# Product-key expert stages on one core: the first head's sixteen experts ranked and fetched as two groups of eight

## What is computed

```python
q = (h @ w_pq).reshape(B, L, PEER_HEADS, 2, PEER_QDIM // 2)
s = jnp.einsum("blhpd,hpkd->blhpk", q, peer_keys)
sv, si = lax.top_k(s, PEER_TOPK)
cand = (sv[..., 0, :, None] + sv[..., 1, None, :]).reshape(B, L, PEER_HEADS, PEER_TOPK * PEER_TOPK)
cidx = (si[..., 0, :, None] * N_KEYS + si[..., 1, None, :]).reshape(...)
top_s, pos = lax.top_k(cand, PEER_TOPK)
eidx = jnp.take_along_axis(cidx, pos, axis=-1)
gate = jax.nn.softmax(top_s, axis=-1)
a = jnp.einsum("tkd,td->tk", peer_down[ee], hh)
act = (gg * jax.nn.gelu(a)).astype(hh.dtype)
return jnp.einsum("tk,tkd->td", act, peer_up[ee])
```

## Time and profile before

| | us |
|---|---|
| three timed runs: median (lowest to highest) | 3960.98 (3959.01 to 3968.05) |
| span of the profiled execution, its own time from first to last instruction | 3961.4 |
| PE busy, matmuls (share) | 3596.4 (91%) |
| DVE busy | 2300.7 (58%) |
| ACT busy | 664.2 (17%) |
| POOL busy | 1284.5 (32%) |
| 16 DMA engines, mean rate | 304 GB/s |

### The profile page before, as it was taken

How to read it: one execution, slowest core, us unless ns; L and a number is a source line. 1 busy time by engine, 2 the same in 40 slices (tenths; PEclk the granted TensorE clock), 3 DMA queues, 4 the chain that set the end, 5 groups by cost and what they waited for, 6 DMA issues and landing times. The chain is left out here.

```text
span 3961.4 us, 41101 instructions
## 1 busy us (share of the span) xinstructions
PE 3596.4 (91%) x14600; PEld 2547.8 (64%) x14600; DVE 2300.7 (58%) x5460; ACT 664.2 (17%) x1814; POOL 1284.5 (32%) x1130
## 2 busy tenths in 40 slices
PE   8998999989999999999999989788779998877777
PEld 6667788878876888888847876333335786433333
DVE  3342013566877887765762147777763226777775
ACT  2232101110001330000002212111112211111111
POOL 1100000023445456774650013444341003444442
PEclk9999999999999999999999999899899999998999
DMA  8752345357998889998983259999996339999997
GB/s 331 291 202 89 128 149 191 128 207 291 345 354 343 292 296 412 406 400 343 414 353 132 102 221 411 398 414 407 411 419 274 108 126 375 405 419 419 420 419 327
DMA packets 206842, 1205.50 MB, mean 304 GB/s; under 512 B 23472, under 2 KB 24640, under 8 KB 95024
## 3 DMA queue, kind: packets, MB, share of 16 engines
q0 software_dynamic: 154976, 858.34, 54.0%
q1 hardware_dynamic: 51664, 344.55, 23.0%
HBM read 1201.64 MB, written 1.15 MB: 304 GB/s over the span
## 5 line engine op out<-in xcount | busy, mean ns | idle before, releaser
L1656 PE MATMUL bank<-big 128*128 128x256 f32 (+4 forms) x8888 | 1909.3, 374 | 47.3 <-DVE big L2435 13.8
L1656 PEld LDWEIGHTS bank<-big 128*128 128x128 f32 (+2 forms) x8888 | 1628.9, 190 | 338.3 <-issue 90.8
L2980 POOL DMA_INDIRECT big<-in_pboth,big x1024 | 1213.2, 1185 | 1301.0 <-PE bank L2134 703.7
L2134 PE MATMUL bank<-big 128*128 128x512 f32 x2048 | 990.6, 641 | 224.7 <-ACT big L2943 224.6
L2635 DVE CUSTOM_DVE_ANT_0 big<-big 128x1024 f32<-128x1024 f32 x768 | 926.1, 1223 | 338.6 <-DMA big<-in_pboth,big 333.2
L2134 PEld LDWEIGHTS bank<-big 128*128 128x128 f32 x2048 | 409.6, 204 | 785.8 <-issue 483.8
L2646 DVE SCALAR_TENSOR_TENSOR big<-big 128x1024 f32<-128x1024 f32 x254 | 326.1, 1284 | 75.7 <-DMA big<-in_pboth,big 55.3
L2967 POOL TENSOR_TENSOR big<-big 128x1 f32<-128x1 f32 (+1 forms) x49 | 42.4, 865 | 914.5 <-DVE big L2192 914.3
L2943 ACT ACTIVATE big<-big 128x128 f32<-128x128 f32 x512 | 165.4, 391 | 270.5 <-DVE big L2612 266.0
L2933 ACT ACTIVATE big<-big 128x4 f32<-128x4 f32 (+2 forms) x136 | 28.1, 207 | 730.9 <-DVE big L2608 725.6
L1836 PE MATMUL bank<-big 128*128 128x256 f32 x576 | 129.5, 378 | 0.0
(11 more groups left out here) (218 smaller groups left out, 2279.7 us busy)
## 6 DMA issues: line engine op xcount, KB each, us to landing
big<-in_w SPq DMA_DIRECT2D x104, 1024.0 KB
big<-in_wmod POOLq DMA_DIRECT2D x48, 1024.0 KB, 8.9
big<-in_wgu SPq DMA_DIRECT2D x44, 1024.0 KB
big<-in_wzg SPq DMA_DIRECT2D x36, 1024.0 KB, 4.8
big<-in_wro SPq DMA_DIRECT2D x32, 1024.0 KB
big<-in_wpq SPq DMA_DIRECT2D x24, 1024.0 KB, 4.9
big<-in_wd SPq DMA_DIRECT2D x22, 1024.0 KB
big<-in_pboth,big POOLq DMA_INDIRECT x1024, 11.0
```

Source lines behind the costliest of these rows:

```text
L1656: last = pe.matmul(o, a, b, start=(i == 0), stop=(i == n - 1))
L2134: last = pe.matmul(u.ap, d.ap, row[:, 512 * i:512 * i + 512], start=(k == 0), stop=(k == 127))
L2980: g.indirect_dma_start(out=s.ap, out_offset=None, in_=table, in_offset=bass.IndirectOffsetOnAxis(ap=index, axis=0)).then_inc(s.full[0], 16)
```

## The change

For head 0 of tile 0 in the expert stages of x (there `GH == 1`; the context's stage has `GH=8` and keeps its order) the 16 experts are ranked in two goes. First the eight best keys of either half are found, then the eight best of their 8 x 8 sums, then the row numbers of these eight, which the fetches of experts 0 to 7 wait for. After that the other eight keys of either half are found, and the sums, the 16 best and their row numbers are made as before; the last eight numbers are written, and the fetch of expert 8 waits for them. One more `next(route)` stands ahead of the steps of L1495, so that all steps of the old order follow as they were, behind the new first one.

```diff
         def rank(tt, h, sc, sc_ok, held=None):
+            eight = GH == 1 and tt == 0 and h == 0
+            keys = [dict(src=sc[:, p, :], vals=rk["sv"][:, p, :], idx=rk["si"].bitcast(U32)[:, p, :]) for p in range(2)]
+            if eight:
+                for p in range(2):
+                    put("rank_eight", ready=sc_ok if p == 0 else None, **keys[p])
+                ix_first.append(tick("index_done"))
+                put("rank_eight_index", rk=rk, dst=eix[0][:, 0, 0:8], done=ix_first[0])
+                yield 5
             for p in range(2):
-                put("rank_keys", src=sc[:, p, :], vals=rk["sv"][:, p, :], idx=rk["si"].bitcast(U32)[:, p, :],
-                    ready=sc_ok if p == 0 else None)
+                put("rank_others" if eight else "rank_keys", ready=sc_ok if p == 0 else None, **keys[p])
                 yield 1.8
             put("rank_pairs", tv=tvs[tt][:, h, :], rk=rk)
             yield 2.6
             ix_ok[tt][h] = tick("index_done")
-            put("rank_index", rk=rk, dst=[e[:, tt, 16 * h:16 * h + 16] for e in eix], done=ix_ok[tt][h])
+            put("rank_index", rk=rk, dst=[e[:, tt, 16 * h:16 * h + 16] for e in eix], done=ix_ok[tt][h], at=8 if eight else 0)
...
         asking = ask()
         route = ranks(asking)
+        next(route)
         next(route)
         r1 = stats(1, self.x_ok)
...
+                new = k % 16 == 0 or (tt, k) == (0, 8)
                 put("fetch", table=t["pboth"], s=s, index=eix[:, tt, k:k + 1],
-                    ready=ix_ok[tt][k // 16] if k % 16 == 0 else None, before=s.before)
+                    ready=ix_first[0] if tt + k == 0 else ix_ok[tt][k // 16] if new else None, before=s.before)
...
+    def rank_eight(src, vals, idx, ready):
+        settled()
+        if ready:
+            v.wait_ge(*ready)
+        step(v.max(vals[:, 0:8], src))
+        settled()
+        step(v.max_index(idx[:, 0:8], vals[:, 0:8], src))
+
+    def rank_others(src, vals, idx, ready):
+        settled()
+        step(v.match_replace(src, vals[:, 0:8], src, -3.0e38))
+        settled()
+        step(v.max(vals[:, 8:16], src))
+        settled()
+        step(v.max_index(idx[:, 8:16], vals[:, 8:16], src))
+
+    def rank_eight_index(rk, dst, done):
+        sv, ab, ia, iot = rk["sv"], rk["ab"][:, :, 0:8], rk["ia"][:, :, 0:8], rk["iot"][:, 0:8]
+        sf, tp = rk["sf"][:, :, 0:8], rk["tp"][:, 0:8]
+        c2 = rk["cand"].rearrange("p a b -> p (a b)")[:, 0:64]
+        oh = rk["oh"].rearrange("p a b -> p (a b)")[:, 0:128].rearrange("p (s k j) -> p s k j", s=2, k=8)
+        best8, abu = rk["ia"][:, 1, 8:16], ab.bitcast(U32)
+        settled()
+        step(v.tensor_tensor(c2.rearrange("p (a b) -> p a b", a=8), bc(sv[:, 0, 0:8], 8), bcm(sv[:, 1, 0:8], 8), ALU.add))
+        step(v.tensor_copy(sf, rk["si"].bitcast(U32)[:, :, 0:8]))
+        settled()
+        step(v.max(best8, c2))
+        settled()
+        step(v.max_index(tp, best8, c2))
+        settled()
+        step(v.tensor_scalar(abu[:, 0, :], tp, 3, None, ALU.logical_shift_right))
+        step(v.tensor_scalar(abu[:, 1, :], tp, 7, None, ALU.bitwise_and))
+        settled()
+        step(v.tensor_copy(ia, abu))
+        settled()
+        v.wait_ge(*rk["iot_ok"])
+        for s in range(2):
+            step(v.tensor_tensor(oh[:, s], bc(ia[:, s, :], 8), bcm(iot, 8), ALU.is_equal))
+        settled()
+        for s in range(2):
+            step(v.tensor_tensor(oh[:, s], oh[:, s], bcm(sf[:, s, :], 8), ALU.mult))
+        settled()
+        for s in range(2):
+            step(v.tensor_reduce(ab[:, s, :], oh[:, s], AX.X, ALU.add))
+        settled()
+        step(v.scalar_tensor_tensor(ia[:, 0, :], ab[:, 0, :], 128.0, ab[:, 1, :], ALU.mult, ALU.add))
+        settled()
+        step(v.tensor_scalar(ia[:, 0, :], ia[:, 0, :], float(16384 * rk["l"]), None, ALU.add))
+        settled()
+        v.tensor_copy(dst, ia[:, 0, :]).then_inc(done[0], 1)
+        v.wait_ge(*done)
+
...
-    def rank_index(rk, dst, done):
+    def rank_index(rk, dst, done, at):
...
-            v.tensor_copy(dst[0], ia[:, 0, :]).then_inc(done[0], 1)
+            v.tensor_copy(dst[0][:, at:16], ia[:, 0, at:16]).then_inc(done[0], 1)
         v.wait_ge(*done)
```

More of the change, by code:

```diff
@@ L1225, in routing @@
                   iot=iot, iot_ok=iot_ok, l=l)
-        ix_ok, gates_ok, ended = [[None] * 8 for _ in range(2)], {}, {}
+        ix_ok, gates_ok, ended, ix_first = [[None] * 8 for _ in range(2)], {}, {}, []
         def rank(tt, h, sc, sc_ok, held=None):
+            eight = GH == 1 and tt == 0 and h == 0
[6 more added lines that the diff above has]
+                yield 5
             for p in range(2):
-                put("rank_keys", src=sc[:, p, :], vals=rk["sv"][:, p, :], idx=rk["si"].bitcast(U32)[:, p, :],
-                    ready=sc_ok if p == 0 else None)
+                put("rank_others" if eight else "rank_keys", ready=sc_ok if p == 0 else None, **keys[p])
                 yield 1.8
@@ L1320, in route @@
             yield from first
-        return route, query, (score_begun, score_end), ranks, ix_ok, gates_ok, ended, query_tile
+        return route, query, (score_begun, score_end), ranks, ix_ok, gates_ok, ended, query_tile, ix_first
     def peer_queries(self, banks, sm, start, size, l, X, vec, ready, indices):
@@ L1355, in peer_c @@
         tvs = [kept.get(128, (8, 16)) for _ in range(2)]
-        route, _, _, ranks, ix_ok, gates_ok, _, _ = self.routing(ar, banks, wr, sm, l, 1, hT, hT_ok, tvs=tvs, gat=gat, eix=eix,
+        route, _, _, ranks, ix_ok, gates_ok, _, _, _ = self.routing(ar, banks, wr, sm, l, 1, hT, hT_ok, tvs=tvs, gat=gat, eix=eix,
                                                               qts=qts, GH=8, kept=kept, **rest)
@@ L1434, in peer_x @@
                              tvs=tvs, gat=gat, eix=[eix], qts=qts, GH=1)
-        _, query, (score_begun, score_end), ranks, ix_ok, gates_ok, ended, query_tile = parts
+        _, query, (score_begun, score_end), ranks, ix_ok, gates_ok, ended, query_tile, ix_first = parts
         yield "alone"
@@ L2676, in final @@
         v.scalar_tensor_tensor(X, X, by, fw, ALU.mult, ALU.mult).then_inc(normed[0], 1)
-    kinds = dict(consts=consts, block_consts=block_consts, row_stats=row_stats, row_turn=row_turn, dt=dt, dt_sums=dt_sums,
+    kinds = dict(consts=consts, rank_eight=rank_eight, rank_others=rank_others, rank_eight_index=rank_eight_index,
+                 block_consts=block_consts, row_stats=row_stats, row_turn=row_turn, dt=dt, dt_sums=dt_sums,
                  conv_in=conv_in, conv_end=conv_end, gate_in=gate_in, group_mask=group_mask, heads=heads, group_gate=group_gate, group_stats=group_stats,
```

## The result

The changed kernel takes **3972.22 us** (median of 15 runs, 3964.96 to 3979.49). The kernel before, run beside it on the same chip, takes 3963.7 (15 runs, 3956.85 to 3971.4). The ratio is **1.0021, 95% interval 1.0014 to 1.0028**: slower by 8.3 us, 5.5 to 11.1. The forecast of 3966.6 and its range up to 3971 were too low.

A forecast was written before the change was run, and what follows sets the result against it. PE was taken to bound about 120 us of each expert stage, started by DVE's ranking of head 0. Two stages at 2.8 us added 5.6, giving 3967.0 profiled, 3966.6 against the timed median; range 3959 to 3971.

The forecast's parts named there:

- the last one of the sum: Both expert stages: PE's run 3.3 us later, about 0.5 us to spare, so transfers 2.8 us later per stage.
- The 0.45 us: Second stage: fetch 46 is used 6.33 us after issue, 0.45 more than fetch 0, taken as its time to spare.
- the early fetches' cost: Start of a stage: fetches keep number, size and order, and the slots they take are free; no cost counted.
- The steps on DVE: Head 0's ranking: split adds nothing, the added index 3.3 us a stage (2.8 to 4.7), moving tile 1 back 3.3.
- What was won early is lost as a longer wait for slots: Expert stages: fetch 0 comes 3.45 us earlier, but later fetches wait for slots PE gives back, so nothing is gained.
- PE is the bound, the transfers follow it: First 120 us or so of a stage: PE has no gap and gives back slots; transfers follow by half a microsecond.
- the two falls of 2 us each: Sign in PE's run: the transfer rate falls to 283 GB/s at 3408 and 221 at 2470, read as transfers barely fed.
- The early start: Rival: transfers bound the whole stage, so each stage ends 3.45 us earlier, giving 3954.1 us; chance 0.08.
- It didn't cancel: Rival on PE's run: fetches have more to spare, for instance 3 us, so lateness cancels, giving 3961 us; chance 0.12.
- PE's clock: Rival: after longer idling PE's full clock returns late, head 1's query loses 3 us a stage, giving 3972.6; chance 0.10.
- a term whose own bounds went to +9.0: Lateness of both stages together: +5.6 us, from +3.2 at the lower price of the added index to +9.0 at the upper.

The follow-up runs named there:

- x1: Changed kernel with the first fetch waiting for head 0's full index, the index of eight still worked out but unused: 3972.46 us, ratio 1.0019.
- x2: Changed kernel with the row numbers of the first eight worked out twice, one after the other: 3977.7 us, ratio 1.0027.
- y1: Changed kernel with tile 1's way out of the banks right behind the first eight keys and the first fetch waiting for the full index: 3967.56 us, ratio 1.0006.
- y2: Kernel before with only tile 1's way out of the banks moved ahead of rank_index; no split ranking, no added instructions: 3968.2 us, ratio 1.0006.
- z2: x3 with the first fetch also waiting for the last DVE instruction of tile 1's way out, for which the query waits too: 3958.36 us, ratio 0.9984.
- x3: Changed kernel with tile 1's root between the eight keys and their index, its way out ahead of the second half's other keys: 3970.79 us, ratio 1.0018.
- z4: x3 with the ninth fetch waiting until tile 1's query on PE is complete, so eight fetches run ahead: 3964.55 us, ratio 1.0003.
- y3: x3 with the first fetch also waiting until tile 1's query on PE is complete: 3966.34 us, ratio 1.0005.
- z1: x3 with the third fetch waiting until tile 1's query on PE is complete, so two fetches run ahead: 3960.02 us, ratio 0.9988.
- z3: x3 with the sixth fetch waiting until tile 1's query on PE is complete, so five fetches run ahead: 3958.37 us, ratio 0.9988.

## Why the prediction was wrong

**The step that failed is the last one of the sum: that a fetch has 0.5 us to spare in each stage, to be taken off the 3.3, and that the transfers are 2.8 us later from there on.** The part before it held: PE's run starts 3.8 and 2.6 us later, 6.5 in all, and 2 x 3.3 was said. At the two fetches the lateness is still the forecast's, by the stages' ends it is not. Timeline of the changed kernel, POOL's fetch 47 of the first stage and DVE's use of it, and DVE's use of fetch 46 of the second; then fetch 46 of the second stage in the second profile of the kernel before:

```profile
2466.59 0.94 POOL L3042 DMA_INDIRECT big<-in_pboth,big  x1 [7.71 <-PE bank L2143]
...
2473.41 1.23 DVE L2696 CUSTOM_DVE_ANT_0 big<-big 128x1024 f32<-128x1024 f32 x1 [0.22 <-DMA big<-in_pboth,big]
...
3416.56 1.23 DVE L2696 CUSTOM_DVE_ANT_0 big<-big 128x1024 f32<-128x1024 f32 x1 [1.49 <-DMA big<-in_pboth,big]
```

```profile
3412.61 0.95 POOL L2980 DMA_INDIRECT big<-in_pboth,big  x1 [7.64 <-PE bank L2134]
...
3419.71 1.22 DVE L2635 CUSTOM_DVE_ANT_0 big<-big 128x1024 f32<-128x1024 f32 x1 [2.18 <-DMA big<-in_pboth,big]
```

Counted from the MAX8, fetch 46 is issued 2.65 us later than before and used 2.88 later; fetch 47 is issued 3.86 later and used 2.97 later. So the two rows are used 2.9 and 3.0 us later, near the 2.8 that were said: 0.9 us was spared in the first stage, nothing in the second. But the lateness doesn't stay so: the ends of the stages come 4.2 and 3.4 us later (5.8 and 2.0 against the second profile of the kernel before), 7.7 in all, more than PE's 6.5. x1 and x2 agree that nothing is left to take off: PE's run starts 5.1 and 12.7 us later there, both stages together, and the stages' sums are 5.5 and 13.1 longer. With nothing taken off, the sum would have been 6.6, beside 8.3 (5.5 to 11.1) by the comparison and 7.7 by the stages' sums. The step was worth 1 us in two stages, so it is the three kernels together that speak against it; one execution alone scatters by more. The 0.45 us was read from one fetch of one execution, and it isn't steady: in the second profile of the unchanged kernel the same fetch is used 7.10 us after its issue, not 6.33. A single late use is no measure of what a whole stretch can spare when its transfers run at 418 to 420 GB/s most of the time.

The rest, 1 us by the stages' sums, stays open. The prediction put the early fetches' cost at nothing, and part of it may be there: in the changed kernel ACT and SP go on 0.7 and 0.6 us behind the end of the query's last row, 1.7 and 1.9 us behind the end of POOL's first burst, and in the kernel before at once. But x1, with no early burst, has 0.7 and 0.2, and the length of one stage moves by more than this from one execution to the next.

The time itself missed by 5.6 us, and half of this is not the change: the kernel before stood at 3960.98 us in the three runs that the forecast rested on, and at 3963.7 in the 15 beside the changed one, of which those three are part. The forecast's 5.6 us on that would have been 3969.3.

**The steps on DVE held.** 3.3 us was forecast for the added index, between 2.8 and 4.7, and 3.22 was measured. Fetch 0 was to come 3.45 us earlier and came 3.69, right behind tile 1's root, as said. Tile 1's query came 3.2 us later, PE had no gap for 122 and 126 us, the rate fell for longer (299 and 335 GB/s over 20 us), and the stages' last fetches were issued 4.2 and 3.4 us later, where nearly 3 was said.

**What was won early is lost as a longer wait for slots:** this held, and x1 shows it: without the early fetch the hole in the rate is gone and the time is not told from the changed kernel's, +7.5 beside +8.3.

**PE is the bound, the transfers follow it** was half of the truth. It holds for a loss: 5.1, 6.5 and 12.7 us that PE's run comes late in x1, the changed kernel and x2 made the stages' sums 5.5, 7.7 and 13.1 longer. It isn't enough for a gain: y1 and y2 start the run 2.9 and 2.7 us sooner in the second stage and are no faster, with the first fetch 4.4 and 1.1 us later. The rates of 406 and 407 GB/s in PE's run, and 418 to 420 in eight of the eleven 20-us stretches from 2362 to 2482 and from 3306 to 3406, spoke for a balance, and the two falls of 2 us each weighed too much.

**The rivals.** The early start didn't carry through. It didn't cancel: the interval begins at 1.0014. PE's clock didn't come back late: the query took 6.74 and 5.49 us of recorded time, against 6.73 and 6.64 before, and head 1's query 7.10 in both stages, as before. The point at which this rival passes 7.9 us was also worked out wrongly: if head 1's query loses half of the delay, 2.3 us more in two stages need a return 2.3 us later, not 1.2. By the Trainium skill, Perfetto Trace Analysis, section Optimization Strategy, one has what the most contended engine waits for start sooner. The runs agree with it only for two engines at once here: the transfers sooner at the cost of PE's start gave +8.3, PE's start sooner at the cost of the first fetch +2.4 (y2, not to be told from nothing), both sooner -6.3 (z2).

**The chances.** Within 0.2% was given 0.76, slower 0.20; 8.3 us lies just above the mark of 7.9, and its interval reaches to both sides of it. The forecast lay 2.3 us below it, with a term whose own bounds went to +9.0, so more of its chance belonged above.

## What to carry to other kernels

Before a stage's first transfer is moved ahead, look at what gives back the buffers: if an engine's own start is late by the work that was put in to make the transfer early, the transfers only wait at another place. Where an engine without gaps and transfers at their full rate stand in the same stretch, move both ends, and price the loss of either in full. A burst of indirect fetches wants a place too: in these kernels it did no harm when it began with the matmuls whose result the next step waits for, or paused before they ended.

## What the runs showed of the chip that was not expected

The completion of a group of matmuls on PE can reach the other engines 6 to 7 us after the group's last row while POOL issues indirect fetches one behind the other. In x3 the burst begins 2.4 us ahead of the group, and ACT and SP go on 1.5 and 1.6 us after the end of POOL's last issue (the tenth, in the first stage the eleventh); in z4 1.2 us after its eighth, in both stages. Where the burst begins 8.3 us ahead, in the changed kernel and in x2, they go on 1.7 to 1.9 us after the burst's end in all four stages, 0.5 to 2.1 us behind the query's last row. With no issue beside the group's end, in y1, y3, z1 and z3, SP goes on within 0.05 us of that row's end; ACT, in most of them, stands behind an instruction of the gates then.

It is not so for every burst: in the kernel before and in x1 the burst begins 1.4 us ahead of the group, in z2 together with it, and the completion comes inside the burst, 6.8 and 6.7 (the kernel before), 6.4 and 5.7 (x1) and 7.2 us (z2) after the group's start, 0.0 to 1.7 us behind its last row. In y2 it begins 3.3 us behind the group's start, and the completion isn't late. What sets this limit between 1.4 and 2.4 us, and which part of the chip holds the signal, no run here shows.
